# Constants of the scan copied ahead of the convolutions, and the squares of x's rows shared by two engines

## The reference, cut to what matters

```python
def rms_norm(x, g):
    xf = x.astype(jnp.float32)
    y = xf * lax.rsqrt(jnp.mean(xf * xf, axis=-1, keepdims=True) + EPS)
    return (y * g.astype(jnp.float32)).astype(x.dtype)

def mamba2_mixer(h, w_in, conv_w, conv_b, dt_bias, A_log, D_skip, g_out, w_out):
    proj = h @ w_in
    z, xBC, dt_raw = jnp.split(proj, [D_INNER, D_INNER + CONV_DIM], axis=-1)
    xBC = jax.nn.silu(causal_depthwise_conv(xBC, conv_w, conv_b))
    xs, Bm, Cm = jnp.split(xBC, [D_INNER, D_INNER + SSM_GROUPS * SSM_STATE], axis=-1)
    dt = jax.nn.softplus((dt_raw + dt_bias).astype(jnp.float32))
    y = ssd_chunked_scan(xh, dt, A, Bm, Cm)     # in it: cum = cumsum(dt * A), L = exp(cum_t - cum_s)
...
```

## Time and profile before

| what | value |
|---|---|
| median of 3 runs | 918.43 us (918.40 to 918.44) |
| profiled execution | 918.89 us |
| its span, first to last instruction | 917.1 us |
| mean granted TensorE clock, share of full speed | 0.998 |
| TensorE busy | 900.9 us, 98% |
| VectorE busy | 594.3 us, 65% |
| ScalarE busy | 486.8 us, 53% |
| GpSimd busy | 116.4 us, 13% |
| DMA share by slices (40 of 22.9 us) | 90% in the first, then mostly 20 to 70% |

### The profile page before, as it was taken

One profiled execution on the slowest core, in us unless ns is written; L12 is line 12 of the kernel. 1 busy time (PEld: TensorE's weight loads), 2 busy tenths in 40 slices (PEclk: granted clock), 3 DMA queues, 4 the chain that ended last, 5 costly groups with the idle time before them and its releaser, 6 DMA issues.

```text
span 917.1 us, 13492 instructions
## 1 busy us (share of the span) xinstructions
PE 900.9 (98%) x4942; PEld 762.5 (83%) x4942; DVE 594.3 (65%) x1082; ACT 486.8 (53%) x795; POOL 116.4 (13%) x110
## 2 busy tenths in 40 slices
PE   9999999999999999999999999999999999999996
PEld 7999878889888879887888888888978788888885
DVE  4898677686768685867655445556685964545454
ACT  4955757567686464764543434325674454334431
POOL 4643864102000010002000000000001100000000
PEclk9999999999999999999999999999999999999999
DMA  9655232573534137332565555544332365555521
GB/s 350 237 194 171 91 123 89 199 259 139 187 128 145 59 112 301 109 122 92 195 238 197 170 212 194 170 152 177 147 138 93 141 225 184 183 187 181 196 80 46
DMA packets 22379, 151.59 MB, mean 165 GB/s; under 512 B 2608, under 2 KB 3120, under 8 KB 4528
## 3 DMA queue, kind: packets, MB, share of 16 engines
q1 hardware_dynamic: 20304, 142.62, 43.4%
q10 hardware_dynamic: 2016, 8.16, 2.4%
HBM read 149.72 MB, written 1.05 MB: 164 GB/s over the span
## 4 chain that ended last, share of the span: by engine, by line
PE 57%; DVE 3%; ACT 2%; issue 1%; POOL 0%; DVEq 0%; POOLq 0%; ACTq 0%
PE ps L516 12%; PE ps L522 12%; PE ps L518 12%; PE ps L1166 5%; PE ps L819 2%; PE ps L821 2%; PE ps L820 2%; PE ps L1184 2%; PE ps L565 1%; PE ps L1228 1%; PE ps L1108 1%; PE ps L549 1%; PE ps L547 1%; PE ps L545 1%; PE ps L861 1%; DVE wlo L1846 1%
## 5 line engine op out<-in xcount | busy, mean ns | idle before, releaser
L1352 ACT CAST whi<-raw 128x2048 fp32r<-128x2048 f32 (+1 forms) x127 | 241.6, 1906 | 141.4 <-PE ps L522 112.5
L1846 DVE TENSOR_TENSOR wlo<-raw,whi 128x1024 fp32r<-128x1024 f32 x127 | 162.3, 1278 | 137.8 <-ACT whi L1352 137.4
L516 PE MATMUL ps<-whi,ahi 128*128 128x512 f32 (+2 forms) x432 | 166.7, 386 | 0.1
L518 PE MATMUL ps<-wlo,ahi 128*128 128x512 f32 (+2 forms) x432 | 165.8, 384 | 0.0
L522 PE MATMUL ps<-whi,alo 128*128 128x512 f32 (+2 forms) x432 | 164.8, 384 | 0.0
L1852 DVE TENSOR_TENSOR wlo<-raw,whi 128x1024 fp32r<-128x1024 f32 x107 | 130.5, 1220 | 0.0
L516 PEld LDWEIGHTS ps<-whi,ahi 128*128 128x128 f32 x432 | 81.1, 188 | 16.9 <-issue 0.9
L522 PEld LDWEIGHTS ps<-whi,alo 128*128 128x128 f32 x432 | 81.1, 188 | 15.8
L518 PEld LDWEIGHTS ps<-wlo,ahi 128*128 128x128 f32 x432 | 81.2, 188 | 15.4
L516 PE MATMUL ps<-whi,bhi 128*128 128x512 f32 x174 | 69.8, 401 | 0.4 <-issue 0.3
L545 PE MATMUL ps<-ahi,whi 128*128 128x256 f32 x240 | 68.4, 285 | 0.0
(11 more groups left out here) (300 smaller groups left out, 1743.6 us busy)
## 6 DMA issues: line engine op xcount, KB each, us to landing
raw<-in_wstream SPq DMA_DIRECT2D x133, 1024.0 KB, 4.8
par<-in_params ACTq DMA_DIRECT2D x5, 1024.0 KB, 4.8
tab<-in_tables ACTq DMA_DIRECT2D x1, 1370.0 KB, 10.0
res<-in_x SPq DMA_DIRECT2D x2, 512.0 KB, 4.6
raw<-in_wstream SPq DMA_DIRECT2D x2, 512.0 KB, 6.4
out<-res SPq DMA_DIRECT2D x4, 256.0 KB, 2.0
par<-in_params ACTq DMA_DIRECT2D x1, 512.0 KB, 4.2
arena<-in_wf ACTq DMA_DIRECT2D x2, 256.0 KB, 5.1
```

The costliest lines, as they stand in the source:

```text
L516: pe.matmul(banks[b][:, 0:cw], h_, wh[:, i, c], start=st, stop=False, skip_group_check=True)
L518: pe.matmul(banks[b][:, 0:cw], h_, wl[:, i, c], start=False, stop=False, skip_group_check=True)
L1352: act.copy(whi[:, u % SPL, c], raw[:, u % RAW, c]).then_inc(w_hi, 1)
L1846: dve.tensor_tensor(wlo[:, u % SPL, c], raw[:, u % RAW, c], whi[:, u % SPL, c].bitcast(F32), ALU.subtract).then_inc(w_lo_v, 1)
```

## The change

Three edits.

1. The squares of x. ScalarE squares columns 0 to 511 of each row (scaled by 1024^-0.5, so that the sum is a mean). VectorE squares columns 512 to 1023 into a sum of its own, `xsq`, both halves of x in front of the first scaling; it waits there for both halves' landing (`x_in`). GpSimd's first instruction adds the two sums and EPS in place of multiplying and adding, and waits for `xsq_done` too.
2. The four constant copies leave `decay_inputs`. They stand in a function `decay_constants`, called once at i = 0, behind `split.until(("bc", 0))` and in front of `convolve(0)`.
3. `cum_done` is raised by the subtraction that was the last step ahead of the copies.

```diff
-            squares(N_X, lambda t: res[:, t, :], D, lambda t: act.wait_ge(x_in[t], 16))
+            squares(N_X, lambda t: res[:, t, 0:512], 512, lambda t: act.wait_ge(x_in[t], 16),
+                    scale=lambda t: D ** -0.5)
...
+            for t in range(T):
+                dve.wait_ge(x_in[t], 16)
+                dve.scalar_tensor_tensor(junk[:, t, 512:D], res[:, t, 512:D], 1.0 / D, res[:, t, 512:D], ALU.mult,
+                                         ALU.mult, accum_out=xsq[:, t:t + 1]).then_inc(xsq_done, 1)
             scale_rows(N_X, lambda t: xn[:, t, :], lambda t: res[:, t, :])
...
+            def decay_constants():
+
+                dve.wait_ge(ident_in, 16)
+                dve.tensor_copy(idr[0:32, :], ident[0:32, 0:32])
+                dve.tensor_copy(idr[64:P, :], ident[64:P, 0:32])
+                dve.tensor_copy(clh[64:P, :], ident[64:P, 0:1].to_broadcast([64, S]))
+                dve.tensor_copy(idr[32:64, :], ident[32:64, 32:64])
+
...
-                dve.tensor_tensor(earg, X[0][:, 64:96], clx[:, 0, 0, :], ALU.subtract)
-                dve.tensor_copy(idr[0:32, :], ident[0:32, 0:32])
-                dve.tensor_copy(idr[64:P, :], ident[64:P, 0:32])
-                dve.tensor_copy(clh[64:P, :], ident[64:P, 0:1].to_broadcast([64, S]))
-                dve.tensor_copy(idr[32:64, :], ident[32:64, 32:64]).then_inc(cum_done, 1)
+                dve.tensor_tensor(earg, X[0][:, 64:96], clx[:, 0, 0, :], ALU.subtract).then_inc(cum_done, 1)
...
             for i in range(12):
                 split.until(("bc", i) if i < 4 else ("xs", i - 4))
+                if i == 0:
+                    decay_constants()
                 convolve(i)
...
             pool.wait_ge(const_set, 1)
-            root(N_X, D)
+            for t in range(T):
+                pool.wait_ge(sq_done, T * N_X + t + 1)
+                pool.wait_ge(xsq_done, t + 1)
+                c = slice(2 * N_X + t, 2 * N_X + t + 1)
+                link(pool.tensor_scalar(ssq[:, c], ssq[:, c], xsq[:, t:t + 1], EPS, ALU.add, ALU.add))
+                pool.tensor_tensor(rstd[:, c], ssq[:, c], neghalf[:, 0:1], ALU.pow).then_inc(rs_done, 1)
```

More of the change, by code:

```diff
@@ L310, in build @@
         lsum = scal(2 * T)
+        xsq = scal(T)
         fsum = scal(2 * T)
@@ L396, in build @@
         y_gated, y_norm = sem("y_gated"), sem("y_norm")
-        fsq = sem("fsq")
+        fsq, xsq_done = sem("fsq"), sem("xsq_done")
         acc_psum, acc_read, lead_t0 = sem("acc_psum"), sem("acc_read"), sem("lead_t0")
```

## The result

| | before | after |
|---|---|---|
| median of six runs, us | 918.47 (918.40 to 918.79) | 922.45 (922.12 to 923.80) |
| ratio, 95% interval | | 1.0046 (1.0035 to 1.0056) |
| profiled execution, us | 918.89 | 922.51 |
| its span, us | 917.1 | 920.7 |
| granted clock, mean | 0.998 | 0.997 |

The changed kernel is slower by 4.0 us, 0.43%. That is outside "within 0.2%", on the slower side, 1.4 us above the forecast of 921.0 and inside the range of 918.5 to 923.0.

The account below looks back on a forecast made before the run. TensorE, busy for 98% of the span, was taken as the bound. +3.1 us at the first convolution and -0.5 at the copies' old place made +2.6, from a median of 918.43 to 921.0 us; range 918.5 to 923.0.

Parts of the forecast that it names:

- Two copies behind two passes: Before convolve(0): two copies each wait for a GpSimd pass, so TensorE's unit 3 starts late, +3.1 us.
- The one that waits is let in when the other ends: VectorE and GpSimd near 26 us: the waiting engine goes next, so two passes hold two copies; the +3.1 us rests on it.
- The rival in which VectorE keeps its turn: Before convolve(0): no pass holds the copies, they cost 0.60 us, the gains stand, -0.6 us, 917.8 us; chance 0.17.
- The rival of one pass: Before convolve(0): only the first copy waits for a pass, unit 3 +1.0 us, in all +0.4, 918.8 us; chance 0.15.
- TensorE's wait: Before unit 3: TensorE waits some 3.7 us for the first convolution, L1999.
- The old place: In front of L685: taking the copies away ends TensorE's wait for L2008, -0.50 us.
- The squares: At the start: sharing them gains TensorE between 0 and 0.23 us, taken as -0.1, ending at unit 3.
- The clock: Behind TensorE's silence at unit 3: clock falls to half, 2.6 us more, 921.0 to 923.6 us; chance 0.06 with two passes.
- Two passes with the fall: At unit 3: two held copies and then TensorE's clock at half, 921.0 to 923.6 us; chance 0.06, without the fall 0.62.

Follow-up runs that it names:

- e1: The changed kernel with the four copies back in `decay_inputs`, so only the squares are shared; 918.86 us against 918.52 before, ratio 1.0003.
- e6: The changed kernel with only the first copy ahead of the first convolution, the other three back in `decay_inputs`; 918.70 us against 918.47 before, ratio 1.0003.
- e4: The changed kernel, but GpSimd waits for the last copy before its pass on unit 3; 918.11 us against 918.52 before, ratio 0.9995.
- e8: The changed kernel with three products of ones keeping TensorE busy in its wait at unit 3; 920.98 us against 918.73 before, ratio 1.0025.
- e2: The kernel before with only the four copies moved, squares left to ScalarE; 922.28 us against 918.52 before, ratio 1.0037.

## Why the prediction was right, and where it was off

**Two copies behind two passes: right, with its times.** First copy forecast near 26.2 with 2.4 us, measured 25.96 with 2.39; second copy 2.4, measured 2.34; three and four below 0.3, measured 0.28 and 0.17. The convolution was forecast for 31.39 and started at 31.10, unit 3 for 33.87 and started at 33.59: a term of +3.1 that measured +2.9. VectorE's tile ahead of the copies came 0.2 earlier than before (24.82, 25.03), where I took 0.1, with up to 0.4 as its bound. "The one that waits is let in when the other ends" was the choice that decided. It holds for the copies in each of these rows, but not for every instruction: GpSimd's TENSOR_SCALAR in e1 was passed over once, as at 164.82. One support of it was misread: the pass of 25.07 did not end 2.40 behind the end of VectorE's tile, which is 25.03 + 1.23 = 26.26, but 2.27 behind it. The rival in which VectorE keeps its turn, 917.8 us, is out. The pass-by-pass price is shown by e6 (one pass: +0.08 at unit 3) and e4 (none). The rival of one pass had +1.0 there, but for all four copies, 0.60 of it for the three that follow the held one; e6 has one copy alone, so it doesn't measure that rival.

**TensorE's wait: right in place, mis-sized.** I expected 3.7 us and it was 2.6 to 2.9. TensorE had the four small transposes of L588, at 30.34, still ahead of it when it was to become idle. The time of unit 3 doesn't depend on that.

**The old place: right, 0.66 for 0.50.** The bracket of 0.50 at L685 was taken as the whole gain. All nine profiles of the table with the four copies moved show 0.66 us from unit 8 to L685 (4.39 to 3.73, 0.00 to -0.66). The bracket didn't hold all that the copies cost there.

**The squares: the lower bound of 0 held, and one cost was missing.** I took -0.1 within 0 and -0.23, and let it end at unit 3. Start and unit 3 are at -0.04 in e1, by the hold of the TENSOR_SCALAR that I had named. The rest of the program I took as untouched; there the squares go with some 0.3 us at 150 us, in all profiles by a race of a few nanoseconds. It would explain that the medians are 4.0 apart and the two profiles 3.6: the profile of before had lost the race already.

**The clock: the step that failed.** The sum without it was +2.6, and e8, where the clock is kept, measured +2.4 in its profile and +2.25 in its median; the two executions of 920.46 and 920.82 are at that place too. They weren't profiled, but their mean granted clock on record is 0.998; the other fourteen of the sixteen with the unfilled wait have 0.994 to 0.997. All three profiles of the unfilled wait (after, twice, and e2) show the fall. I gave it a chance of 0.06, because "the longest wait inside is 0.7 us" and no row showed what follows a longer one. That was the absence of evidence taken for evidence, and the evidence was there: TensorE is also silent at the end of the kernel, and the same trace of before has, for its last product and two stretches behind it,

```profile
909.51 0.39 PE L821 MATMUL ps<-whi,blo 128*128 128x512 f32 x1
...
910.00:914.28 4.28, 0.00 (x0) 0.00 (x0) 3.30 (x7) 1.24 (x2) 0.79 (x2) 1.00 0.00 0
914.28:917.10 2.82, 0.00 (x0) 0.00 (x0) 0.37 (x1) 0.00 (x0) 0.00 (x0) 0.50 0.50 186
```

The clock fell 4.4 us behind the last product, a silence not much longer than the 3.7 us that I forecast. The start showed that TensorE can stand at half clock, and the Trainium skill's "TensorE: Matmul & The Clock Gate", Part 1, said that idleness leads there, with which these rows agree. Its price was off the other way in two of three: half of 5.3 us, 2.6, carried over from the start; measured are 1.46, 1.48 and 2.65. Two passes with the fall would have had to be the likeliest case, and with the commoner loss of 1.5 the forecast would have been 922.5. The range held the time only since it reached into this case. That the change would be slower by more than 0.2% didn't need the clock: e8, without the fall, is 2.25 us above before, outside the 1.8 us of 0.2%.

The account of the medians: +2.93 at unit 3, +1.46 by the clock, -0.66 at the old place, -0.11 from there to the end of the two profiles, make 3.62; what is left to 4.0 is the 0.4 by which the profile of before lies above its own median. I put it down to the race, which no run shows for the executions that weren't profiled.

## What to carry to other kernels

A small copy on VectorE can cost as much as the GpSimd instruction beside it, whatever its own size: look at what GpSimd runs or is about to run at the place, and count one held copy for each pass that is ready, as the waiting pass came in behind the copy here. Put such copies where VectorE idles longer than one pass afterwards; ahead of the one tile that TensorE will wait for, they are dear even though each looks like 0.2 us. When a sum yields a new wait for a busy TensorE that is longer than any in the trace, price what comes behind the wait too, as a likely case and not as a remainder; and when a filler is to tell wait and clock apart, take its duration from a row of the same shape. Products of ones stood at the start of the trace of before, 0.43 us apart at full clock and two rows for each.

## What the runs showed of the hardware that was not expected

- After a silence of 2.61, 2.77 or 2.87 us the granted clock fell from 1.00 to 0.50 in all three executions profiled with it: once 0.76 us before the work resumed, once 0.16 and once 0.96 us behind. It stayed there for 3.41 us twice and for 6.83 once. With products in the silence and 0.34 us of wait left it didn't fall. The loss varies from one execution to the next (1.46 to 2.65 us), which also makes the times of such a kernel spread: 2.8 us, against 0.4 without the fall.
- VectorE and GpSimd can change over at the boundary between two instructions, even if the next one of the same engine follows without a gap: the second copy came behind the second pass. It is no strict turn: in e1 GpSimd's one-column TENSOR_SCALAR stood through two scalings of VectorE (0.67 us), at 164.82 in the kernel before for 1.99 us. Some nanoseconds can decide it: at 150 us, a lead of 27 to 29 ns and one of 17 to 26 ns made 0.19 or 0.76 us of the same instruction, and 0.4 us on TensorE.
- A product of f32 with 512 columns stands as two matmul rows of 0.44 us each (24 rows for 12 products, 10.57 us), where products of float32r parts with 512 columns (L819 to L821 at 909 us in the kernel before) stand one row each and 0.23 us apart.
